# Router logits from stationary weights in four column groups, and four smaller edits, in a one-core encoder kernel

## The reference

```
x  = LN0(x)
mix = concat(latent attention, 8 heads; differential attention, 4 heads) @ w_o
x1 = LN1(alpha*x + mix)
scores = sigmoid(x1 @ w_router)              # 16 experts in 4 groups
top group by its best two; top two experts inside it; gates from the scores
y  = sum over chosen experts of gate * (silu(x1@w_gate[e]) * (x1@w_up[e])) @ w_down[e]
out = LN2(alpha*x1 + y)
```

## Time and profile before

| | |
|---|---|
| median of 3 runs | 786.39 us (784.81 to 787.71) |
| profiled execution, own time | 789.17 us |
| its span | 785.9 us (3.3 us lie around it) |
| mean granted PE clock | 0.977 |
| busy: PE, DVE, ACT, POOL | 94%, 74%, 62%, 34% |

### The profile page before, as it was taken

One profiled execution on the slowest core, in us unless ns is written; L12 is line 12 of the kernel. 1 busy time (PEld: TensorE's weight loads), 2 busy tenths in 40 slices (PEclk: granted clock), 3 DMA queues, 4 the chain that ended last, 5 costly groups with the idle time before them and its releaser, 6 DMA issues.

```text
span 785.9 us, 12710 instructions
## 1 busy us (share of the span) xinstructions
PE 737.5 (94%) x3844; PEld 613.3 (78%) x3844; DVE 582.2 (74%) x975; ACT 483.5 (62%) x874; POOL 265.9 (34%) x291
## 2 busy tenths in 40 slices
PE   4999999999999799999999899999999999999984
PEld 3898888888887577768787677888877777777862
DVE  6965365557555766684878799889988888889657
ACT  3334355557554745675137277788888878888635
POOL 3132356656664333344311114222222222222111
PEclk9999999999999789999998999999999999999998
DMA  9724311222144933321745759999999999999763
GB/s 342 251 108 134 120 58 44 61 68 68 37 133 141 324 155 121 122 75 46 298 173 207 260 195 397 392 370 381 387 372 388 378 374 377 384 388 377 250 214 160
DMA packets 71484, 179.35 MB, mean 228 GB/s; under 512 B 11687, under 2 KB 28071, under 8 KB 71444
## 3 DMA queue, kind: packets, MB, share of 16 engines
q1 hardware_dynamic: 66692, 166.34, 56.0%
q0 software_dynamic: 4752, 12.51, 6.4%
HBM read 153.20 MB, written 30.42 MB: 234 GB/s over the span
## 4 chain that ended last, share of the span: by engine, by line
PE 58%; DMA 19%; DVE 11%; ACT 5%; issue 3%; POOL 2%; SPq 1%; ACTq 0%; DVEq 0%; POOLq 0%
PE bank L649 34%; DMA rawG<-in_w_gate 16%; PE bank L1777 4%; PE bank L1779 3%; PE bank L1778 3%; DVE eGl L1932 2%; PE bank L784 2%; DMA wv_raw<-in_w_in 2%; PE bank L1800 1%; PE bank L1798 1%; PE bank L1799 1%; PE bank L2157 1%; ACT eGh L1862 1%; DMA dv_l<-dv_low 1%; POOL me L1269 1%
## 5 line engine op out<-in xcount | busy, mean ns | idle before, releaser
L1932 DVE TENSOR_TENSOR eDl<-rawD,eDh 128x1024 fp32r<-128x1024 f32 x68 | 80.2, 1219 | 12.3 <-ACT eDh L1862 12.1
L1269 POOL TENSOR_SCALAR me<-me,mrec 128x512 f32<-128x512 f32 (+1 forms) x48 | 65.6, 1368 | 52.2 <-DVE mrec L1448 52.1
L1932 DVE TENSOR_TENSOR eUl<-rawU,eUh 128x1024 fp32r<-128x1024 f32 x68 | 78.8, 1219 | 2.6 <-ACT eUh L1862 2.6
L1932 DVE TENSOR_TENSOR eGl<-rawG,eGh 128x1024 fp32r<-128x1024 f32 x64 | 75.5, 1220 | 5.9 <-ACT eGh L1862 5.0
L2055 POOL DMA_INDIRECT acc_rows<-yg,idx_s x16 | 29.7, 1858 | 135.5 <-ACT yg L1887 135.5
L1862 ACT ACTIVATE eGh<-rawG 128x1024 fp32r<-128x1024 f32 x64 | 65.7, 1058 | 7.4 <-DMA rawG<-in_w_gate 6.9
L1862 ACT ACTIVATE eDh<-rawD 128x1024 fp32r<-128x1024 f32 x64 | 64.0, 1055 | 0.0
L1777 PE MATMUL bank<-eGh,xgT_h 128*128 128x512 f32 x136 | 55.9, 411 | 8.5 <-DVE xgT_l L1937 7.4
L1862 ACT ACTIVATE eUh<-rawU 128x1024 fp32r<-128x1024 f32 x64 | 62.8, 1052 | 0.0
L1777 PE MATMUL bank<-eUh,xgT_h 128*128 128x512 f32 x136 | 54.6, 401 | 0.0
L1779 PE MATMUL bank<-eGl,xgT_h 128*128 128x512 f32 x136 | 53.3, 392 | 0.0
(11 more groups left out here) (346 smaller groups left out, 2185.4 us busy)
## 6 DMA issues: line engine op xcount, KB each, us to landing
rawG<-in_w_gate SPq DMA_DIRECT2D x68, 512.0 KB, 15.5
rawU<-in_w_up SPq DMA_DIRECT2D x68, 512.0 KB, 12.2
rawD<-in_w_down SPq DMA_DIRECT2D x68, 512.0 KB, 13.6
wb_raw<-in_w_in SPq DMA_DIRECT2D x8, 512.0 KB, 4.6
wo_raw<-in_w_o SPq DMA_DIRECT2D x8, 512.0 KB, 7.6
xln_rows<-res SPq DMA_DIRECT2D x6, 512.0 KB, 3.8
dqk_high<-st_h SPq DMA_DIRECT2D x8, 384.0 KB, 2.3
dqk_low<-st_l SPq DMA_DIRECT2D x8, 384.0 KB, 3.3
```

The costliest lines, as they stand in the source:

```text
L1269: nc.gpsimd.tensor_scalar(e, e, mrec[:, g % NSB:g % NSB + 1], None, ALU.mult).then_inc(m_p, 1)
L1932: nc.vector.tensor_tensor(wl_[X][i][:], raw_of(X, t, i)[:], f32(wh_[X][i][:]), ALU.subtract).then_inc(s_lo[X], 1)
```

## The change

1. **Unread products** in slots z = 0, 1, 2 of differential attention: 6, 10 and 4 products of 512 columns into bank 3, ahead of everything else in the slot.
2. **Router logits**: the router weights, widened with 16 columns of zeros to 32, are now the stationary operand, and the turned x1 (128 columns) streams. Chunk c writes to partitions 32j to 32j+31 with j = c mod 4, so four column groups of the array are used in turn (`part_sums`). ACT copies the 128x128 partial sums out, and one product with a matrix `fold` (two identities stacked per 32 rows) sums the groups and turns the result (`logits`). Tile t alternates between banks 2 and 3; the exponential becomes two. POOL prepares `fold` and the zeros. The order on ACT around it changes.
3. **Statistics by halves**: DVE takes the statistics of half 0 right after its add. The low parts of G units 0 and 1 of tile 0 move in behind the first half of tiles 4 and 5.
4. **Fill products** ahead of the prefix sum: 16 in place of 11.
5. **Expert orders**: ACT does `rows(t-1)` after the high parts of D units 0, 1 and the x copy of the next tile; DVE does the x low part between D units 0 and 1; D of tile 0 is made low before G of tile 1.
6. One semaphore serves both norm weights, and one small tile moves.

```diff
+    UNREAD = {0: 6, 1: 10, 2: 4}
...
+        def unread_products(n):
+            for _ in range(n):
+                nc.tensor.matmul(psum[3][:], mixM_h[:, 0, 0:P], mixM_h[:, 1, 0:512], start=True, stop=True)
         def diff_slot(z):
+            if z == 0:
+                pe.wait_ge(m_ptl, MT)
+                pe.wait_ge(m_mh, HEADS)
+            if z in UNREAD:
+                unread_products(UNREAD[z])
...
@@ experts, ACT
             if not last:
                 high("G", t + 1)
-            rows(t - 1)
             high("D", t, (0, 1))
             if not last:
                 x_high(t + 1, 0)
+            rows(t - 1)
@@ experts, DVE
-            if first_iteration(t):
-                low_part("D", 0, (0, 1))
-                h_low(0)
-                low_part("D", 0, (2, 3))
-            else:
+            if not first_iteration(t):
                 low_part("D", t - 1, (2, 3))
-                h_low(t - 1)
+            h_low(t - 1)
...
-            low_part("D", t, (0, 1))
+            low_part("D", t, (0,))
             if not last:
                 x_low(t + 1, 0)
+            low_part("D", t, (1,))
...
         low_part("U", 0, (1, 2, 3))
+        low_part("D", 0)
         low_part("G", 1)
@@ logits, PE
-            def logits(t):
-                pe.wait_ge(s_x1e, 2 * t + 2)
-                pe.wait_ge(s_rt, 32)
-                pe.wait_ge(s_y, 12)
-                for c in range(KD):
-                    last = nc.tensor.matmul(psum[2][:, t * NE:(t + 1) * NE], x1T[t % 2][:, c, :], wr_sb[:, c, :],
-                                            start=(c == 0), stop=(c == KD - 1))
+            def part_sums(t):
+                pe.wait_ge(s_x1e, 2 * t + 2)
...
+                for c in range(KD):
+                    j = c % 4
+                    last = nc.tensor.matmul(psum[2 + t % 2][2 * NE * j:2 * NE * (j + 1), 0:P], wr_sb[:, c, :],
+                                            x1T[t % 2][:, c, :], start=(c < 4), stop=(c >= 4))
+                last.then_inc(s_log, 1)
+            def logits(t):
+                pe.wait_ge(s_part, t + 1)
+                nc.tensor.matmul(psum[2 + t % 2][:, P + t * NE:P + (t + 1) * NE], part_logits[t % 2][:], fold[:, 0:NE],
+                                 start=True, stop=True).then_inc(s_log, 1)
...
-                logits(t - 3)
+                part_sums(t - 3)
+                if t > 3:
+                    logits(t - 4)
                 turn_x1(t - 2)
-            turn_x1(NT - 2)
-            logits(NT - 3)
-            turn_x1(NT - 1)
-            logits(NT - 2)
-            logits(NT - 1)
+            turn_x1(4)
+            part_sums(3)
+            logits(2)
+            part_sums(4)
+            logits(3)
+            turn_x1(5)
+            part_sums(5)
+            logits(4)
+            logits(5)
...
-            keep_busy(11)
+            keep_busy(16)
@@ logits, ACT
-            for t in range(4):
-                x1_turned(t)
-                if t == 3:
-                    x1_turned(4)
-                x1_scaled(t)
-                if t < 3:
-                    act.wait_ge(s_o, 12)
-                    high0("G", (t,))
+            def part_copied(t):
+                act.wait_ge(s_log, parts_done(t))
+                nc.scalar.activation(part_logits[t % 2][:], psum[2 + t % 2][:, 0:P], ACT.Copy).then_inc(s_part, 1)
+            x1_turned(0)
+            for t in range(3):
+                x1_scaled(t)
+                act.wait_ge(s_o, 12)
+                high0("G", (t,))
+                part_copied(t)
+                x1_turned(t + 1)
+            x1_turned(4)
+            part_copied(3)
+            x1_scaled(3)
+            part_copied(4)
             act.wait_ge(s_o, 24)
             high0("G", (3,))
             x1_turned(5)
+            part_copied(5)
             x1_scaled(4)
@@ POOL
+            nc.gpsimd.memset(wr_sb[:, :, NE:2 * NE], 0.0)
+            done(nc.gpsimd.tensor_tensor(i64[:], ident[:, 0:P // 2], ident[:, P // 2:P], ALU.add))
+            done(nc.gpsimd.tensor_tensor(fold[:], i64[:, 0:2 * NE], i64[:, 2 * NE:4 * NE], ALU.add))
@@ x1, DVE
-                dve.wait_ge(s_y, 12 + 2 * t + 1)
-                nc.vector.bn_stats(stats[:, t % 2, 0, :], res[:, t, 0:HW])
-                dve.wait_ge(s_y, 12 + 2 * t + 2)
-                then(nc.vector.bn_stats(stats[:, t % 2, 1, :], res[:, t, HW:D]))
+                    dve.wait_ge(s_y, 12 + 2 * t + hf + 1)
+                    last = nc.vector.bn_stats(stats[:, t % 2, hf, :], res[:, t, ns])
+                    if hf == 0 and t >= 4:
+                        g0_low(t - 4)
+                then(last)
```

More of the change, by code:

```diff
@@ L415, in encoder_trunk @@
     BF = mybir.dt.bfloat16
-    wr_sb = tmp("wr_sb", [P, KD, NE])
+    wr_sb = tmp("wr_sb", [P, KD, 2 * NE])
+    fold = tmp("fold", [P, 2 * NE])
     br_sb = tmp("br_sb", [P, NE])
@@ L421, in encoder_trunk @@
     i32a = tmp("i32a", [P, P], I32)
+    i64 = at("i64", 207, [P, P // 2])
     itile = tmp("itile", [P, MAX_TILES])
@@ L455, in encoder_trunk @@
     idx_f = tmp("idx_f", [P, MAX_TILES])
-    le = tmp("le", [1, MAX_MORE + 1, NE])
+    le = at("le", 173.125, [1, MAX_MORE + 1, NE])
     te_f = tmp("te_f", [1, MAX_TILES])
@@ L468, in encoder_trunk @@
     n_more_sb = small("n_more_sb", [1, 1], I32)
[L470 removed]
+    s_lnw, s_rt = sem("norm_weights_landed"), sem("router_weights_landed")
     s_x1 = sem("x1_ready")
@@ L475, in encoder_trunk, with parts_done, logits_done @@
     s_consts = sem("router_constants")
+    part_logits = [at(f"part_logits{i}", 206 + 0.5 * i, [P, P]) for i in range(2)]
+    s_part = sem("part_logits_copied")
+    def parts_done(t):
+        return max(1, 2 * t)
+    def logits_done(t):
+        return min(2 * t + 3, 2 * NT)
     s_rexp, s_member, s_prefix = sem("router_exp"), sem("router_members"), sem("router_prefix")
@@ L2020, in experts_dve @@
         nc.vector.tensor_scalar_add(mv[:, 0, 1:2], mv[:, 0, 1:2], LN_EPS).then_inc(s_var, 1)
-        dve.wait_ge(s_ln2w, 32)
+        dve.wait_ge(s_lnw, 64)
         for t in range(NT):
@@ L2126, in _ @@
             sp.wait_ge(s_o, 24)
-            sp.wait_ge(s_log, NT)
+            sp.wait_ge(s_log, 2 * NT)
             for i in range(4):
@@ L2150, in turn_x1 @@
                     last.then_inc(s_x1t, 1)
-            def logits(t):
-                pe.wait_ge(s_x1e, 2 * t + 2)
-                pe.wait_ge(s_rt, 32)
-                pe.wait_ge(s_y, 12)
-                for c in range(KD):
-                    last = nc.tensor.matmul(psum[2][:, t * NE:(t + 1) * NE], x1T[t % 2][:, c, :], wr_sb[:, c, :],
-                                            start=(c == 0), stop=(c == KD - 1))
-                last.then_inc(s_log, 1)
+            def part_sums(t):
+                pe.wait_ge(s_x1e, 2 * t + 2)
+                if t == 0:
+                    pe.wait_ge(s_rt, 32)
+                    pe.wait_ge(s_consts, 1)
+                    pe.wait_ge(s_y, 12)
+                    pe.wait_ge(s_otl, DT)
+                for c in range(KD):
[3 more added lines that the diff above has]
+                last.then_inc(s_log, 1)
+            def logits(t):
+                pe.wait_ge(s_part, t + 1)
+                nc.tensor.matmul(psum[2 + t % 2][:, P + t * NE:P + (t + 1) * NE], part_logits[t % 2][:], fold[:, 0:NE],
+                                 start=True, stop=True).then_inc(s_log, 1)
             for k in range(16, 18):
@@ L2222, in x1_turned @@
                     act.wait_ge(s_x1t, 2 * t + hf + 1)
-                    wait(act, s_log, t - 1)
+                    if t >= 2:
+                        act.wait_ge(s_log, parts_done(t - 2))
                     nc.scalar.activation(x1T[t % 2][:, 4 * hf:4 * hf + 4, :],
@@ L2246, in _ @@
             x1_turned(5)
+            part_copied(5)
             x1_scaled(4)
-            act.wait_ge(s_log, NT)
-            nc.scalar.activation(sg[:], psum[2][:, 0:NT * NE].rearrange("p (t e) -> p t e", t=NT), ACT.Exp,
-                                 scale=-1.0).then_inc(s_rexp, 1)
+            act.wait_ge(s_log, 2 * NT)
+            for i in range(2):
+                logit = psum[2 + i][:, P:P + NT * NE].rearrange("p (t a e) -> p t a e", a=2, e=NE)[:, :, i, :]
+                nc.scalar.activation(sg[:].rearrange("p (t a) e -> p t a e", a=2)[:, :, i, :], logit, ACT.Exp,
+                                     scale=-1.0).then_inc(s_rexp, 1)
             x1_scaled(5)
@@ L2315, in _, with g0_low @@
             front_dve(dve)
-            dve.wait_ge(s_ln1w, 32)
+            dve.wait_ge(s_lnw, 32)
+            def g0_low(i):
+                dve.wait_ge(s_hi["G"], i + 1)
+                nc.vector.tensor_tensor(wl_["G"][i][:], raw["G"][i][:], f32(wh_["G"][i][:]), ALU.subtract).then_inc(s_lo["G"], 1)
             for t in range(NT):
@@ L2333, in _ @@
                                                op0=ALU.mult, op1=ALU.add).then_inc(s_x1, 1)
-            for i in range(4):
-                dve.wait_ge(s_hi["G"], i + 1)
```

(5 more changed lines are left out.)

11 lines of the change are left out of this document (5 added, 6 removed).

## The result

The changed kernel took 778.62 us (median of 4 runs, 777.22 to 779.4) against 787.0 (784.81 to 787.71) for the kernel before on the same chip: a ratio of 0.9879, 95% interval 0.9851 to 0.9907. A second comparison, of 6 and 11 runs, gave 0.9865 (0.9841 to 0.989). The profiled execution took 779.4 us, with a span of 777.6 and a mean granted clock of 0.987 in place of 0.977. The forecast was 777.5.

The account below looks back on a forecast made before the run. Bounds: half clock at differential attention's start and the logits, transfers in the experts. 789.17 - 4.6 - 3.5 + 0.1 - 1.5 = 779.7 us profiled; 8.9 of 9.5 taken off the 786.39 median gives 777.5, range 771 to 784.5.

Parts of the forecast that it names:

- part 1: Start of differential attention: unread products keep PE's clock full, DVE and ACT become the bound; -4.6 us, ends -6.7 and +3.7.
- part 3: First expert iteration: D of tile 1 loads in the transfer hole, later loads start earlier; -1.5 us, ends -5 and +1.
- Part 2: Router logits in column groups, statistics by halves and longer fill; -3.5 us, ends +1.5 and -5.5.
- milestones of the tail: After the last projection half ends at T: last turn T+5.3, x1 copied T+7.2, DVE's first router step T+9.5 us.
- wholly side by side: Router logits: a tile's sums if all column groups overlap fully, 0.43 us; serial 1.72, and 0.96 was counted.
- ends of this part: Logits' bounds: loop -2.1 and +0.4, tail -3.5 and 0, fill up to +1.5 us late; summed as +1.5 and -5.5.
- The gather: Experts: moving `rows` issues scatter and gather 2.5 us later, slack falls from 3.3 to 0.8 us; cost nothing.
- R3: Experts: gather late, PE waits 0.3 us in 14 iterations, +4, 781.5 us; decides once landing passes 9 us; chance 0.10.
- R1: Differential attention: clock stays up but DVE and ACT hold slots 1 to 3; -1.6 for -4.6, 780.5 us; chance 0.17.
- R2: Logits: column groups don't run side by side, or each change drains; -0.5 us there, 780.5 us total; chance 0.14.
- R4: First expert iteration: the transfer hole is won whole; 774 us; chance 0.10.
- R5: Clock is down when unread and fill products are issued, slots and routing run late; 790 us; chance 0.07.

Follow-up runs that it names:

- pairs of one group: Changed kernel with a tile's eight sum products issued as pairs of one column group (0, 0, 1, 1, ...) instead of in turn: 779.46 us, ratio 0.9877.
- measure run: The changed kernel run again unedited, as the measure for the follow-up kernels: 778.06 us, ratio 0.9865 to the kernel before.
- early gather: Changed kernel with POOL starting a tile's gather one iteration earlier, ahead of the previous tile's add of the rows: 778.01 us, ratio 0.9868.
- rows back: Changed kernel with ACT scaling the rows ahead of D's high parts again, as in the kernel before: 778.38 us, ratio 0.9872.
- one column group: Changed kernel with all eight products of a tile's sums added up in one column group instead of four: 785.39 us, ratio 0.9966.

## Why the prediction was right

**The total.** 8.9 us were forecast, 8.4 and 10.3 measured in the two comparisons. It was put together from terms of which two were off in opposite ways, part 1 too large and part 3 too small, so that it came so near is in part luck. The three parts taken out one by one add up to 9.9 by the ratios (3.4, 3.5, 3.0), where the whole is 10.6.

**Part 1** (-4.6). The mechanism was right: full clock, unread products in the idle time, DVE and ACT as the next bound (0.68 us of waiting for `o_sb` at 275.3 where 275.2 was forecast for slot 3). The term was too large: slot 4 came 4.2 earlier, and the part alone is worth 3.5. About 1 us of the 4.2 is the clock's fall in that one execution of before (slot 0 to 4: 21.9 there, 20.9 without the unread products).

**Part 2** (-3.5). 3.6 by the kernel without it (2.2 to 2.6 by its own chip), 3.3 by the first router step less part 1 (7.5 - 4.2). The milestones of the tail came out at T+5.5, T+7.4 and T+9.5, where T+5.3, T+7.2 and T+9.5 stood. Two steps inside were wrong, and cancelled, which is luck. I counted 0.96 for a tile's sums, on the view that two instructions of a group follow each other and only neighbours lie side by side: it is 0.58, the pairs of one group show that the order does not count, and what is left without the change of mode (0.41) is the 0.43 that I had called wholly side by side. And I gave the halves of the statistics 0.6: they are worth nothing at the turn, since the early low part (1.2 us) and the half statistics do not fit into the idle time of DVE once the loop is tighter (1.40 us there, 2.04 before). The Trainium skill ("TensorEngine Tiling (Array Packing)", Key Properties) says that changing the tiling mode drains TensorE. The trace agrees as far as it goes: some 0.26 us a tile for the change and back, read above, where the estimate in the prediction was 0.1 and the sum itself had nothing; no run parts the change of mode from the other shape of the products. The fill products cost nothing, as said (1.79 us of PE's idle time is left behind them). The ends of this part are added up a little wrong: +0.4, 0 and +1.5 make +1.9 and not +1.5, and -2.1 and -3.5 make -5.6. The forecast does not use them.

**Part 3** (-1.5). Too small, most likely: 2.4 to 3.8 by the times, with 1.5 inside their intervals. The step that failed is "my count leaves a queue shorter by about 1.5 us". U of tile 2 alone goes out 2.6 us later without the edit, and 1.2 MB more are left at 720 (window 720:785: 202 GB/s, and 184 in the measure run), 3.1 us at 381 GB/s. That the 2 MB of D moved ahead of the stretch count beside the issue of U is how I read it; no run parts the two.

**The gather** (0, "with the least cover of all edits"). The rival R3 came true as an event, at 8.6 to 8.8 us a little before its 9, and not as a cost: 3.3 us of waits, nothing in the time, since the two kernels without these waits (early gather, rows back) took as long. R1 did not come about beyond 1 us of part 1; R2 is refuted by the one column group, though a change of mode has a price; R4 is half true, in that the hole was worth more than 1.5 by the medians, though it moved and did not close. R5 fell with the clock at full in 264 to 282.

**Not foreseen:** the clock's fall at the experts' start (0.50 all through 434 to 440 here, 0.72 in the measure run). No run took it away: where the clock held until 449, it fell right behind, so its price is not shown.

## What to carry to other kernels

When a long stretch is full of transfers, price an edit ahead of it by the transfers that it moves out of the stretch (the bytes left at 720 followed the spans within 1.2 us here), and read a new wait inside it as a symptom until an experiment has removed it: the gather's was removed in two ways here, and neither moved the time. An edit that keeps the clock up in one window has to be checked in the next ones too, since the fall can move there. Small outputs of a long sum are worth putting in four column groups; exchanging stationary and moving side without the groups is a loss. And a step whose sum comes out right can hold two errors that cancel; a run of each piece tells.

## What the runs showed of the hardware that was not expected

Sixteen instructions (eight float32 products of 128 columns, 32-column weights) take 0.65 us in four column groups, 0.66 with neighbours in the same group, and 1.93 in one group. Going from 128 columns of weights to 32 and back went with about 0.26 us more (0.09 in front, 0.17 up to the next turn). With 20 unread products in PE's idle time the clock stayed full from 260 to 290 us, where without them it fell ahead of slot 1 and PE then worked 15 us at a mean of 0.61. An indirect gather in full transfers took 7.9 us to land (median) when it was issued 3.5 us after a scatter, 8.6 at 2.8 us after it, and 7.6 (up to 9.7) when it was issued ahead of it.
